# Moving a modulation gate from the combine stage into the expert blocks' PSUM eviction

## The reference, cut to what matters

```python
hl2 = modulate(rmsnorm(xl, norm_ffn[i]), mod_l[3], mod_l[4])   # i = 1, the last layer
xl = xl + mod_l[5] * moe(hl2, *moe_prm)                        # mod_l[5]: 1024 numbers, one per channel
return rmsnorm(xl, norm_f)

# moe: every token goes to two of 16 experts; e is an expert, xb a block of 128 tokens, g their gates
hid = jax.nn.silu(xb @ w1[e]) * (xb @ w3[e])                   # 1024 -> 512
y   = (hid @ w2[e]) * g[:, None]                               # 512 -> 1024; the two y of a token are added
```

## Time and profile before

| | us |
|---|---|
| median of 3 runs | 1663.09 |
| the profiled execution: device time | 1661.36 |
| its span, first to last instruction | 1659.6 |
| layer 1's expert blocks in it | about 1291 to 1625 |
| layer 1's combine stage in it | about 1627 to 1656.5 |
| PE / DVE / ACT busy over the span | 1404.1 / 1110.0 / 714.7 |

### The profile page before, as it was taken

The page is one execution under the profiler, slowest core; times in us unless marked ns, Lnnn a source line. Parts: engine busy times, 40 slices in busy tenths (PEclk is TensorE's granted clock), DMA queues, the critical chain, the costliest instruction groups (busy, mean ns, idle before and its releaser), DMA issues. The chain is left out here.

```text
span 1659.6 us, 20694 instructions
## 1 busy us (share of the span) xinstructions
PE 1404.1 (85%) x6750; PEld 985.6 (59%) x6751; DVE 1110.0 (67%) x1473; ACT 714.7 (43%) x823; POOL 167.3 (10%) x144
## 2 busy tenths in 40 slices
PE   3888989547976999999998299799996799999980
PEld 2445555224445788888887244378653577777770
DVE  2179999984776886596552452366556688888834
ACT  3200101041344775576552330166433477777732
POOL 0000000000321021010110200000001121112101
PEclk9899999778987999999999599899997799999995
DMA  9358357209007997799574600040161799999924
GB/s 336 107 186 288 134 192 263 114 6 338 39 27 271 360 399 269 278 400 387 202 265 152 261 1 0 20 83 2 36 231 58 273 363 399 396 398 398 395 102 190
DMA packets 164095, 357.57 MB, mean 215 GB/s; under 512 B 7776, under 2 KB 35152, under 8 KB 164048
## 3 DMA queue, kind: packets, MB, share of 16 engines
q1 hardware_dynamic: 147520, 301.31, 49.9%
q0 software_dynamic: 8784, 31.99, 5.1%
q10 hardware_dynamic: 7744, 23.68, 3.6%
HBM read 318.57 MB, written 38.37 MB: 215 GB/s over the span
## 5 line engine op out<-in xcount | busy, mean ns | idle before, releaser
L702 DVE TENSOR_TENSOR W_LO<-W_RAW,W_HI 128x2048 fp32r<-128x2048 f32 x192 | 432.9, 2287 | 140.9 <-ACT W_HI L695 119.8
L695 ACT ACTIVATE W_HI<-W_RAW 128x2048 fp32r<-128x2048 f32 x192 | 362.4, 1912 | 94.2 <-DMA W_RAW<-in_moe_w 50.1
L1395 PE MATMUL PS<-W_HI,XLO 128*128 128x512 f32 x624 | 251.3, 403 | 23.7 <-DVE XLO L1529 23.7
L1397 PE MATMUL PS<-W_HI,XHI 128*128 128x512 f32 x624 | 245.7, 394 | 0.0
L1396 PE MATMUL PS<-W_LO,XHI 128*128 128x512 f32 x624 | 245.3, 393 | 0.0
L1175 PE MATMUL PS<-HT,RING 128*128 128x512 f32 (+1 forms) x512 | 173.6, 495 | 6.8 <-DVEq L1246 6.8
L1395 PEld LDWEIGHTS PS<-W_HI,XLO 128*128 128x128 f32 x624 | 118.8, 190 | 53.9 <-issue 22.8
L1175 PEld LDWEIGHTS PS<-HT,RING 128*128 128x128 f32 x512 | 96.9, 193 | 86.2 <-issue 72.5
L1395 PE MATMUL PS<-W_HI,HLO 128*128 128x512 f32 x312 | 126.0, 404 | 9.5 <-DVE HLO L1541 9.5
L1397 PEld LDWEIGHTS PS<-W_HI,XHI 128*128 128x128 f32 x624 | 118.7, 190 | 25.8
L1396 PEld LDWEIGHTS PS<-W_LO,XHI 128*128 128x128 f32 x624 | 118.9, 191 | 23.1
(11 more groups left out here) (237 smaller groups left out, 1810.2 us busy)
## 6 DMA issues: line engine op xcount, KB each, us to landing
W_RAW<-in_moe_w SPq DMA_DIRECT2D x192, 1024.0 KB, 11.1
RING<-in_w_mod SPq DMA_DIRECT2D x24, 2048.0 KB, 14.5
moe_out<-YO ACTq DMA_DIRECT2D x39, 512.0 KB, 6.2
moe_out<-HT SPq DMA_DIRECT2D x20, 512.0 KB, 8.4
RING<-in_conv_pw SPq DMA_DIRECT2D x16, 512.0 KB, 5.3
ROWS<-rows_of_layer SPq DMA_DIRECT2D x12, 512.0 KB, 6.0
RING<-in_attn_w_qkv SPq DMA_DIRECT2D x3, 2048.0 KB, 8.2
moe_in<-RING SPq DMA_DIRECT2D x10, 512.0 KB, 3.0
```

Source lines behind the costliest of these rows:

```text
L695: nc.scalar.activation(part(W_HI[q], p), part(WRAW[q], p), ACT.Copy).then_inc((w2_hi if q == 2 else w_hi)[L], 1)
L702: nc.vector.tensor_tensor(part(W_LO[q], p), part(WRAW[q], p), part(W_HI[q], p).bitcast(F32), ALU.subtract).then_inc(lo[L], 1)
L1395: pe.matmul(to, lo, W_HI[q][:, at:at + 512], start=start, stop=False)
L1397: return pe.matmul(to, hi, W_HI[q][:, at:at + 512], start=False, stop=stop)
```

## The change

Layer 1 only. The modulation vector m is loaded at the start of the expert blocks into GROW, a free part of the HT tile (a table of zeros, NIL, is moved in the same tile to make room). The copy of a block's result out of PSUM, an ACT instruction, becomes a DVE multiply by GROW (`y_gate`). In DVE's step it stands between the split of w3 and the split of w2; ACT then waits for it (`ya_ready`) before it issues the DMA of the result. DVE's step 2 is written out ahead of its loop. In the combine stage the two choices are added straight into x by two DVE instructions (x = g1 c1 + x, x = g2 c2 + x); ACT's multiply by g1 and DVE's multiply by m are gone, and SP no longer loads m at the end of layer 1's blocks. Layer 0 keeps its instructions.

```diff
--- before.py
+++ after.py
@@ -202,6 +202,7 @@
         LANE = table(2 * TILES, P)
         BLOCK = table(2 * TILES, DEEP[0] * NE)
         LOGT = table(2, P)
+        NIL = table(256)
         R, SELM = table(TILES, NE), table(TILES, NE)
         R8 = table(TILES, 8)
         CUM = table(TILES + 1, NE)
@@ -214,8 +215,8 @@
         SHIFTS, SCR2 = (table(NE) for _ in range(2))
         OVER = table(NE * TILES)
         OF = table(2)
-        NIL = table(256)
         assert at[0] <= KT * TOK
+        GROW = HTF[:, 4096:4096 + D]
         assert 2 * KT * P + 2 * TILES * (P + DEEP[0] * NE) >= 4096
         rowsd = [dram(f"rows_of_layer{L}", [2 * NMOD, D]) for L in range(2)]
         h2d = [dram(f"moe_in{L}", [TOK, D]) for L in range(2)]
@@ -1342,6 +1343,8 @@
                 @block.sync
                 def _(sp):
                     n = blocks(sp)
+                    if L == 1:
+                        sp.dma_start(GROW, rowsd[L][NMOD + 5, :].partition_broadcast(P)).then_inc(gates_in[L], 16)
 
                     load_weights(sp, L, 1, (0, 1))
                     for e in range(2, NE):
@@ -1357,8 +1360,8 @@
                     rows = sp.compute_val(n * 16)
                     sp.wait_ge(y_out[L], rows)
 
-                    load_row(sp, L, 1, 5, 5, gates_in[L])
                     if L == 0:
+                        load_row(sp, L, 1, 5, 5, gates_in[L])
                         load_row(sp, L, 0, 5, 4, gates_in[L])
                         load_qkv(sp, 1)
                     else:
@@ -1480,11 +1483,12 @@
                                              ACT.Copy).then_inc(hT_ready[L], 1)
 
                     def y_store(b, rows):
-                        act.wait_ge(w2_used[L], b + 1)
-                        if not first(b):
-                            act.wait_ge(y_out[L], b * 16)
-                        nc.scalar.activation(YO[:, :].rearrange("p (a n) -> p a n", a=2), PS[:, 5:7, :],
-                                             ACT.Copy).then_inc(ya_ready[L], 1)
+                        if L == 0:
+                            act.wait_ge(w2_used[L], b + 1)
+                            if not first(b):
+                                act.wait_ge(y_out[L], b * 16)
+                            nc.scalar.activation(YO[:, :].rearrange("p (a n) -> p a n", a=2), PS[:, 5:7, :],
+                                                 ACT.Copy).then_inc(ya_ready[L], 1)
                         act.wait_ge(ya_ready[L], b + 1)
                         act.dma_start(yd[L][rows, :], YO[:, :]).then_inc(y_out[L], 16)
 
@@ -1536,6 +1540,15 @@
                             dve.wait_ge(hid_turned[L], b)
                         nc.vector.tensor_tensor(HID[:, :], PU3, SIL[:, :], ALU.mult).then_inc(hid_ready[L], 1)
 
+                    def y_gate(b):
+
+                        dve.wait_ge(w2_used[L], b + 1)
+                        if not first(b):
+                            dve.wait_ge(y_out[L], b * 16)
+                        nc.vector.tensor_tensor(YO[:, :].rearrange("p (a n) -> p a n", a=2), PS[:, 5:7, :],
+                                                GROW.rearrange("p (a n) -> p a n", a=2),
+                                                ALU.mult).then_inc(ya_ready[L], 1)
+
                     def hid_lo(b):
                         dve.wait_ge(hT_ready[L], b + 1)
                         nc.vector.tensor_tensor(HLO[:, :, :], PHB.rearrange("p (k n) -> p k n", k=4),
@@ -1553,12 +1566,16 @@
                         hid(b - 1)
                         x_lo(b)
                         split_new(before, load, 1)
+                        if L == 1 and not (isinstance(b, int) and b == 1):
+                            y_gate(b - 2)
                         if isinstance(b, int) and b == 1:
                             split_lo(dve, L, 0, 2)
                         else:
                             split_new(load_of(dve, b - 2), before, 2)
                         hid_lo(b - 1)
 
+                    if L == 1:
+                        dve.wait_ge(gates_in[L], 16)
                     block_step(1)
 
                     st = Steps(dve, dve_step, dve_n[0])
@@ -1582,12 +1599,19 @@
                     st(nc.vector.tensor_copy(DST[:, :, c], DSTF[:, :, c]))
                     dve_n[0] = st.n
 
-                    with dve.Fori(2, n) as b:
+                    block_step(2)
+                    with dve.Fori(3, n) as b:
                         block_step(b)
                     last = last_block(dve)
                     hid(last)
+                    if L == 1:
+                        but_one = dve.value_load(INFO[0:1, LAST_BUT_ONE:LAST_BUT_ONE + 1], min_val=NE - 2,
+                                                 max_val=nb - 2)
+                        y_gate(but_one)
                     split_new(load_of(dve, last - 1), load_of(dve, last), 2)
                     hid_lo(last)
+                    if L == 1:
+                        y_gate(last)
 
 
         combine_norm = [(sq_done[1], ms_ready[1], rms_ready[1]), (f_sq[1], f_ms[1], f_rms[1])]
@@ -1606,7 +1630,7 @@
             sq, _, rms = combine_norm[L]
             nc.scalar.activation(spare[:, :], ones[:, 0:1], ACT.Sqrt)
             for i in range(len(tiles) + 2):
-                if i < len(tiles):
+                if i < len(tiles) and L == 0:
                     act.wait_ge(choices_in[i], 32 * (L + 1))
                     nc.scalar.activation(choice(2 * i), choice(2 * i), ACT.Copy,
                                          scale=GATE[:, 0, i:i + 1]).then_inc(c1_gated[L], 1)
@@ -1626,9 +1650,19 @@
             sq, ms, rms = combine_norm[L]
             st = Steps(dve, dve_step, dve_n[0])
             dve.wait_ge(gates_in[L], 32)
+
+            def add_choice(i, c):
+
+                x = X[:, tiles[i], :]
+                return nc.vector.scalar_tensor_tensor(out=x, in0=choice(2 * i + c), scalar=GATE[:, c, i:i + 1], in1=x,
+                                                      op0=ALU.mult, op1=ALU.add)
+
             for i in range(len(tiles) + 2):
                 c1, c2 = (choice(2 * i + c) if i < len(tiles) else None for c in range(2))
-                if i < len(tiles):
+                if i < len(tiles) and L == 1:
+                    dve.wait_ge(choices_in[i], 32 * (L + 1))
+                    st(add_choice(i, 0))
+                elif i < len(tiles):
                     dve.wait_ge(choices_in[i], 32 * (L + 1))
                     dve.wait_ge(c1_gated[L], i + 1)
                     st(nc.vector.scalar_tensor_tensor(out=c1, in0=c2, scalar=GATE[:, 1, i:i + 1], in1=c1,
@@ -1638,7 +1672,9 @@
                     dve.wait_ge(sq, 2 * base + i)
                     nc.vector.tensor_scalar(ss[:, t:t + 1], ss[:, t:t + 1], 1.0 / D, EPS, ALU.mult,
                                             ALU.add).then_inc(ms, 1)
-                if i < len(tiles):
+                if i < len(tiles) and L == 1:
+                    add_choice(i, 1).then_inc(x_done[L], 1)
+                elif i < len(tiles):
                     st(nc.vector.tensor_tensor(c1, c1, ROWS[:, 4 + stream(tiles[i]), :], ALU.mult))
                     nc.vector.tensor_tensor(X[:, tiles[i], :], X[:, tiles[i], :], c1, ALU.add).then_inc(x_done[L], 1)
                 if 1 <= i <= len(tiles):
```

## The result

The changed kernel takes 1682.74 us, the median of four runs (1681.32 to 1684.29), the kernel before 1663.28 us over four runs. The ratio is 1.0123 with a 95% interval of 1.01 to 1.0146: slower by some 20 us, where 1683 had been forecast. The profiled execution took 1681.32 us, with a span of 1679.6 us.

The account below looks back on a forecast made before the run. DMA bounds the 18.46 us step; after the change a DVE-ACT ring of 20.14 us does. Blocks +23.3, exit +1.8, last results +0.4, SP -0.3, combine stage -4.9: +20.3, forecast 1683 us, range 1674 to 1692.

Parts of the forecast that it names:

- What bounded before: Layer 1's expert blocks: weights' arrival by DMA sets the 18.46 us step; PE alone needs 17.67 us.
- The ring: Layer 1's blocks: DVE's multiply and ACT's wait form a cycle of six start-to-start pieces, 20.14 us a step against 18.46.
- The sixth: Layer 1's step: high part of w2 to the low part of the next w1, all contiguous, 7.01 us.
- rival A: Layer 1's blocks: multiply fits DVE's 1.13 us idle time, ACT's wait is absorbed, step stays 18.46; median 1658; chance 0.08.
- Entry and exit: Ends of layer 1's blocks: +3.5 us up to block 3's XLO; +1.8 us at the exit, +0.4 for last results.
- PE's wait ahead of each down product: Layer 1's steps: PE waits about 1.8 us for HLO ahead of each down product.
- The DMA share: Layer 1's steady steps: DMA share falls to near 0.95 from 1.04.
- The combine stage: After the blocks: removed ACT and DVE instructions shorten DVE's chain, -4.9 us net, bounds -3.5 and -6.
- what would be given back: Combine stage: 0.6 us for tile 1's late choices and some 0.3 for adds waiting for each other.
- rival C: PE in layer 1: clock falls cost 1.5 us each; median 1685 to 1692; chance 0.06.
- The rule cited: PE's clock: frequent short idles between matmul groups can make it swing between two levels; counted against a clock of 1.00.
- rival D: Layer 1's weight loads: still late, each step gains up to 1 us; 1695 us; chance 0.05.

Follow-up runs that it names:

- e7: The kernel before with layer 1's weight loads cut to half their bytes from expert 1 on: 1656.14 us, ratio 0.9954, step 17.70 us.
- e1: The changed kernel with the multiply one place earlier in DVE's step, ahead of the low parts of w3: 1658.54 us, ratio to before 0.9972.
- e2: The changed kernel with ACT's wait for the multiply and the result's DMA issue moved behind the high parts of w2: 1659.47 us, ratio to before 0.9973.
- e4: The changed kernel with a second multiply of the same size and source ahead of each y_gate: 1701.1 us, ratio to before 1.0226.
- e3: The changed kernel without the multiply in the expert blocks, ACT copying the result as before; new combine stage kept: 1656.64 us, ratio to before 0.9963.
- e6: The changed kernel with layer 1's weight loads cut to half their bytes from expert 1 on: 1681.28 us, ratio to before 1.0112.

## Why the prediction was right

- **What bounded before.** Weights first, PE close behind: shown by e7 (18.46 to 17.70, forecast 17.67 from layer 0).
- **The ring.** Forecast 20.14 from six start-to-start pieces, measured 20.07. Five are within 0.03 us: XLO to w3 1.13, two splits 4.40, multiply 1.21, end of the eviction to w2 1.36 (1383.06 - 1381.70), low part to XLO 5.00. The sixth, from w2's high part to the next w1's low part, is 6.96 for 7.01. One step of the reasoning was wider than the ring is. The prediction puts SIL, HHI and the next w1 split of ACT into it, and the rows show them off it: HHI ends at 1387.74 and is used at 1389.42, and the first half of w1's high part, some 1.9 us from 1387.63, is in before DVE takes it up at 1390.02, straight from HLO. ACT's share of the ring is only the 3.3 us from the multiply's end (1381.70) to the low part of w2 (1385.01): the DMA issue, what follows it, and half of a split. The price came out right because the piece was measured to DVE's rows, where it is half a split of ACT and then DVE's own work. The ring is shown as the cause by e1 and e2, which open it at two different places, and by e4, which lengthens it by the full start-to-start time of what is added.
- **The cover named in rival A.** DVE's 1.13 us of idle time was there in the kernel before, but the wait that counted is ACT's, 7.25 us a step. (The 3.4 us by which the eviction ends later are 3.3 by the prediction's own figures.) With the multiply one place earlier, in e1, rival A does hold: 1658.5 us, where A had 1658.
- **Entry and exit.** Entry +3.0 for +3.5, exit +2.3 for +2.2. PE's wait ahead of each down product was sized at 1.8 us and is 1.4. The DMA share was to be near 0.95 and is 0.99.
- **The combine stage.** -5.5 for -4.9. The term that was off is what would be given back: 0.6 for tile 1 and 0.3 for adds that wait for each other, against 0.28 measured for tile 1. e3 shows the gain by itself.
- **The clock (rival C).** It stayed at 1.00 in all 12 steps of the changed kernel, at waits of 1.4 and 0.5 us a step. The rule cited (the Trainium skill, TensorE: Matmul & The Clock Gate, A second HAM failure mode) is borne out only where the waits grow to 2.5 us (e4). There, as reckoned, a fall is hidden by the ring in the steady part, and where it is not, at the exit, the first one costs 1.4 us for the 1.5 of the prediction.
- **Late weights (rival D).** Refuted by e6: half the bytes, and the step stays at 20.06 us.
- **Luck in the total.** 1.8 us of the profiled difference lie ahead of the change and happen to offset what I had too much in the entry and the steps (1.4) and too little in the combine stage's gain (0.6). Without them the trace gives +18.2 for my +20.3. The medians, at +19.5, do not depend on that one execution, but they too hold the scatter ahead of the blocks; that 1683 was met to within 0.3 us is luck, and the sizes are right to about 2 us.

## What to carry to other kernels

When work moves from one in-order engine to another, its price is first a matter of its place in the receiving engine's list, and of what stands behind the wait that the giving engine is left with. Only once the two lists form a ring that sets the step does its duration count, and then in full (e4). Add up the cycle through both lists start to start, from a step in which nothing else is late, and compare it with the present step; slack of both engines (2.6 and 4.3 us a step here) says nothing as long as each waits for the other. Put such an operation where its input is ready and its consumer still busy: here one place earlier turned a loss of 20 us into a gain of 5, which is the combine stage's.

## What was not expected of the hardware

ACT's next w1 split starts 0.48 us behind the start of HHI (1387.15 to 1387.63), where the step of layer 0 that the earlier trace rows begins had 0.96 between the same two (717.65 to 718.61). The profile calls the 0.37 us of idle time there "issue"; what makes the difference no run shows. It costs the changed kernel nothing, since DVE does not wait for that split. And PE's clock, at waits of 2.5 us in the steps of 21.2 us of e4, fell behind six and not behind two (1458.46 full, 1628.08 half), while waits of 1.1 to 1.8 us in the same stage never lowered it.
